# Row biases added on VectorE, a gating norm later in a bit search, and the first weight tiles of blocks three and four multiplied among the closing norms before them

## What is computed

```python
# block two (hybrid_layer)
proj = x @ w_in + b_in          # one bias per output column
ya = spatial_gating(gelu(a_u), gelu(a_v), a_ln_g, a_ln_b, a_ws, a_bs)   # layer norm of a_v over 256 columns
yc = dsa_attention(...)         # keeps the 256 best keys of each query (top_k), then softmax
km, vm = split(mem @ w_mem_kv, 2)
y = mixed @ w_out + b_out
x = layer_norm(DEEPNORM_ALPHA * x + y, ln_g, ln_b)
# block three: y = block(x @ w_in_3 ...) @ w_out_3;  x = layer_norm(ALPHA * x + y, ln1_g, ln1_b)
# feed-forward: a width-3 causal convolution over x @ w_up, gelu, product, @ w_down, layer norm
```

## Time and profile before

| | |
|---|---|
| three timed runs | 3071.8, 3079.6, 3080.2 us, median 3079.6 |
| profiled execution | 3074.3 us, its span 3072.2 us |
| TensorE busy in the span | 2867.8 us (93%), mean granted clock 0.975 |
| VectorE, ScalarE, GpSimd busy | 1721.1, 913.6, 554.6 us |

### The profile page before, as it was taken

How to read it: one execution, slowest core, us unless ns; L and a number is a source line. 1 busy time by engine, 2 the same in 40 slices (tenths; PEclk the granted TensorE clock), 3 DMA queues, 4 the chain that set the end, 5 groups by cost and what they waited for, 6 DMA issues and landing times. The chain is left out here.

```text
span 3072.2 us, 34403 instructions
## 1 busy us (share of the span) xinstructions
PE 2867.8 (93%) x13624; PEld 2299.5 (75%) x13624; DVE 1721.1 (56%) x2463; ACT 913.6 (30%) x1304; POOL 554.6 (18%) x274
## 2 busy tenths in 40 slices
PE   6899999999999999999998888999889999998997
PEld 3688888878887776678855677878677888886775
DVE  2699998655537642776987675782652233221032
ACT  2111112143324332322166512773411222212221
POOL 0000000000100010002100002442004443334664
PEclk9999999999999999999989899999999999999998
DMA  6111222224244530101110221001221111112342
GB/s 257 62 49 59 92 89 62 96 93 144 90 158 124 171 124 28 55 28 48 35 46 15 90 89 59 31 25 28 103 89 48 48 48 48 48 48 81 117 130 96
DMA packets 86643, 242.05 MB, mean 79 GB/s; under 512 B 6818, under 2 KB 33826, under 8 KB 84212
## 3 DMA queue, kind: packets, MB, share of 16 engines
q1 hardware_dynamic: 81620, 222.17, 21.9%
q10 hardware_dynamic: 4640, 17.30, 1.5%
q0 software_dynamic: 256, 0.82, 0.1%
HBM read 206.71 MB, written 33.55 MB: 78 GB/s over the span
## 5 line engine op out<-in xcount | busy, mean ns | idle before, releaser
L294 PE MATMUL pair<-u_hi,w_hi 128*128 128x512 f32 x768 | 300.7, 392 | 12.5 <-DVE w_lo L567 12.2
L516 DVE SCALAR_TENSOR_TENSOR conv_acc<-aT,cols,conv_acc 128x1024 f32<-128x1024 f32 x232 | 297.8, 1284 | 6.8
L296 PE MATMUL pair<-u_hi,w_lo 128*128 128x512 f32 x768 | 299.6, 390 | 0.0
L295 PE MATMUL pair<-u_lo,w_hi 128*128 128x512 f32 x768 | 299.5, 390 | 0.0
L294 PE MATMUL pair<-h_hi,up_hi 128*128 128x512 f32 x704 | 275.1, 391 | 7.4 <-POOL up_lo L289 7.4
L295 PE MATMUL pair<-h_lo,up_hi 128*128 128x512 f32 x704 | 274.8, 390 | 0.0
L296 PE MATMUL pair<-h_hi,up_lo 128*128 128x512 f32 x704 | 274.8, 390 | 0.0
L2564 DVE SCALAR_TENSOR_TENSOR ua<-pair,cols,ua 128x1023 f32<-128x1023 f32 x44 | 56.4, 1282 | 340.8 <-ACT ua L2548 340.8
L294 PEld LDWEIGHTS pair<-u_hi,w_hi 128*128 128x128 f32 x768 | 144.7, 188 | 43.5 <-DVE w_lo L567 12.4
L1663 DVE TENSOR_SCALAR_CACHE_REDUCE counted<-choice,top_i 128x384 uint8<-128x384 f32 (+2 forms) x192 | 168.9, 942 | 0.1
L295 PEld LDWEIGHTS pair<-u_lo,w_hi 128*128 128x128 f32 x768 | 144.7, 188 | 30.4 <-issue 0.5
(11 more groups left out here) (387 smaller groups left out, 6378.9 us busy)
## 6 DMA issues: line engine op xcount, KB each, us to landing
wt<-in_w_ch SPq DMA_DIRECT2D x60, 512.0 KB, 3.6
wo_raw<-in_w_out SPq DMA_DIRECT2D x48, 512.0 KB, 3.6
wt<-in_w_up SPq DMA_DIRECT2D x44, 512.0 KB, 3.4
wt<-in_w_down SPq DMA_DIRECT2D x44, 512.0 KB, 3.6
ada<-in_ada_w SPq DMA_DIRECT2D x8, 1536.0 KB, 8.0
wt<-in_w_conv SPq DMA_DIRECT2D x16, 512.0 KB, 3.6
qk<-qk_st SPq DMA_DIRECT2D x8, 1024.0 KB, 6.3
gates<-qk_st ACTq DMA_DIRECT2D x16, 512.0 KB, 2.6
```

The lines of the kernel that those rows point to most:

```text
L294: nc.tensor.matmul(bank, w[0], x[0], start=(first and k == 0), stop=False)
L295: nc.tensor.matmul(bank, w[0], x[1], start=False, stop=False)
L296: return nc.tensor.matmul(bank, w[1], x[0], start=False, stop=(last and k == n_k - 1))
L516: nc.vector.scalar_tensor_tensor(dst, x, w, conv_acc[:], ALU.mult, ALU.add).then_inc(conv_step, 1)
```

## The change

It has four parts.

1. **Row biases.** The 16 matmuls L1474 are gone. `b_row` is loaded to all 128 partitions, and VectorE takes each bank out with an addition of the bias. The eight of step 0 stand ahead of the logits, the eight of step 1 in the bit search, at places of the list `ROWS_AT` (two per search step: behind the third count and behind the sixth). ScalarE's copies are gone, and its Gelu stands behind the memory copies.
2. **Search.** `gate_norm` stands after step 22, the gating products after steps 29 and 30, and all 36 tie operations ahead of the attention.
3. **Block three.** `project_out` returns its engine programs; they run in the same block as the next stage. Behind the transposes of token tile 6, TensorE multiplies the first half (tokens 0 to 511) of weight tiles 0 and 1, into `pair[3]` and `pair[0]`; then come the transposes of token tile 7, then the second halves. The splits of these two weight tiles stand in the closing norm of block two: high on ScalarE ahead of its token loop, low on GpSimd. The block's end, the clearing of semaphores and the barriers between are gone; the pairs of the tiles of block three and the order of its last token tiles (`I_ORDER`) follow.
4. **Feed-forward.** The same with the first two tiles of `w_up`; GpSimd makes both of their parts during the closing norm of block three. Tiles 2 and 3 are written out ahead of the loops. The load of tile 3 waits until tile 1 is finished, since the low part of tile 1 lies in its slot.

```diff
+                if tail:
+                    pe.wait_ge(res_ok, TT - 1)
+                    pe.wait_ge(lo_ok, TT // 2)
+                    tail[0](pe)
                     if hT is not None:
                         transposes(TT - 1)
+                if tail:
+                    pe.wait_ge(lo_ok, TT)
+                    tail[1](pe)
...
-            sp.dma_start(b_row[:], a["b_row2"]).then_inc(b_in, 16)
+            sp.dma_start(b_row[:], bcast(a["b_row2"], 0, N_R2)).then_inc(b_in, 16)
...
-        N_TIES, TIES_AHEAD = 6 * (TT - 2), 24
+        N_TIES, TIES_AHEAD = 6 * (TT - 2), 36
...
-                    nc.tensor.matmul(bank, ones_row[:], b_row[:, c0:c1], start=False, stop=True).then_inc(row_mm, 1)
+                    last.then_inc(row_mm, 1)
...
+            ROWS_AT = [2, 4, 5, 6, 7, 9, 10, 11]
...
+            def row_evacuation(step, t):
+                c0, c1 = row_columns(1 - step)
+                j = step * TT + t
+                dve.wait_ge(row_mm, j + 1)
+                nc.vector.tensor_tensor(row2[:, t, c0:c1], row_bank(j)[:, 0:c1 - c0], b_row[:, c0:c1],
+                                        ALU.add).then_inc(row_ok, 1)
...
                 for t in range(2, TT):
                     count(n + 1, t, cand[:, t - 2:t - 1].bitcast(F32), ALU.is_ge)
+                    if t in (4, TT - 1) and 2 * n + (t > 4) in ROWS_AT:
+                        row_evacuation(1, ROWS_AT.index(2 * n + (t > 4)))
...
-                if n == 12:
+                if n == 22:
                     gate_norm()
-                if n in (26, 28):
-                    gate_product((n - 26) // 2)
+                if n in (29, 30):
+                    gate_product(n - 29)
...
-        clear_semaphores(keep=p3_w)
...
+                def first_tokens(pe):
+                    for w in range(2):
+                        pe.wait_ge(w3_lo, w + 1)
+                        for i in range(KT):
+                            tile_step(w, i)
+
+                def last_tokens(pe):
+                    for w in range(2):
+                        for i in range(KT, 2 * KT):
+                            tile_step(w, i)
+
+                second_out[1](pe, tail=(first_tokens, last_tokens))
...
+                third_out[0](sp)
+                for n in (2, 3):
+                    sp.wait_ge(*((up_split, 3) if n == 2 else (up_mm, 4)))
+                    sp.dma_start(wt[:, n % 2, :, :], a["w_up"][n, :, :].rearrange("p (k c) -> p k c", k=KT))\
+                        .then_inc(up_w[n % 2], 16)
...
+                for n in range(4):
+                    w_hi, w_lo = up_first[n] if n < 2 else [x[:, n % 2, :, :] for x in up_parts]
+                    pool.wait_ge(up_w[n % 2], 16 * (n // 2 + 1))
+                    if n >= 2:
+                        pool.wait_ge(third_mm, TT)
```

More of the change, by code:

```diff
@@ new lines, in evacuate, with run_scalar @@
+            def evacuate(act, t):
+                act.wait_ge(tr_mm, t + 1)
+                nc.scalar.activation((hT[0] if parts else hT)[:, :, t * P:(t + 1) * P],
+                                     flat(pair[2]).rearrange("p (k s) -> p k s", s=P), ACT.Copy).then_inc(tr_ok, 1)
+            def run_scalar(act, ahead=None):
+                for i, (to, src) in enumerate(vecs):
+                    act.dma_start(to[:], bcast(src, 0, D)).then_inc(vec_in, 16)
+                if split:
+                    act.wait_ge(*early)
+                    for n, k in enumerate(w_order):
+                        for i in range(len(w_loads)):
+                            if n == w_loads[i][2]:
+                                act.wait_ge(out_w[i], 16)
+                        nc.scalar.activation(split["w"][0][:, k, :], w_tile(k), ACT.Copy).then_inc(part_hi, 1)
+                        nc.scalar.activation(split["x"][0][:, k, :], split["raw"][:, k, :], ACT.Copy)\
+                            .then_inc(part_hi, 1)
+                if ahead:
+                    ahead(act)
+                for t in range(TT):
+                    if first_norm:
+                        act.wait_ge(res_ok, t + 1)
+                        nc.scalar.activation(tmp[:], xt[:, t % ring, :], ACT.Square, accum_out=sq_).then_inc(rms_sq, 1)
+                        act.wait_ge(rms_sq, t + 1)
+                        nc.scalar.activation(sd, sq_, ACT.Sqrt, bias=eps6[:], scale=1.0 / D).then_inc(norm_sd, 1)
+                    act.wait_ge(norm_in, t + 1)
+                    nc.scalar.activation(sd, mv_[:, 1:2], ACT.Sqrt, bias=eps5[:]).then_inc(norm_sd, 1)
+                    if t and hT is not None:
+                        evacuate(act, t - 1)
+                if hT is not None:
+                    evacuate(act, TT - 1)
@@ L1669, in mix_vector @@
             row_low(0, 1)
+            dve.wait_ge(b_in, 16)
+            dve.wait_ge(h2_out[0], 48)
+            dve.wait_ge(h2_out[1], 48)
+            for t in range(TT):
+                row_evacuation(0, t)
             dve.wait_ge(row_ok, TT)
@@ L2350, in _ @@
             def _(dve):
+                second_out[3](dve)
                 own = Count(dve, lb_dve)
```

373 lines of the change are left out of this document (188 added, 185 removed).

## The result

| | before | changed |
|---|---|---|
| timed runs, median | 3079.9 us (4 runs, 3071.8 to 3081.6) | 3023.6 us (4 runs, 3022.4 to 3026.4) |
| ratio | | 0.983, 95% interval 0.9817 to 0.9843 |
| span of the profiled execution | 3072.2 us | 3021.4 us |

A forecast was written before the change was run, and what follows sets the result against it. TensorE was taken as the bound, busy 2867.8 of 3072.2 us. Terms 16.8 + 3.7 + 2.8 + 16.0 + 15.0 - 1.5 - 1.5 = 51.3 off 3074.3 gave 3023.0; 2.7 for the executions' middle made 3026 us, range 3016 to 3043.

The forecast's parts named there:

- Row biases: Row steps 0 and 1: without the bias matmuls each of 16 row tiles falls by 1.05 us, 16.8 us won.
- Gelu: Ahead of the memory keys: ScalarE's activation moved behind the memory copies shortens TensorE's gap and avoids low clock, 3.7 us won.
- Ties: Attention's first items: VectorE's tie operations no longer hold up five items, which took 13.16 us instead of 10.35; 2.8 won.
- VectorE is not what ends here.: Search: VectorE's 47 us of saved waiting turn into only 2.8 us, since TensorE does not directly wait for it.
- Ends of the blocks: Ends of blocks two and three: first halves between token tiles 6 and 7's transposes win 16.0 and 15.0 us.
- Clock: The 2.46 us gap at each of two block ends: granted clock may fall behind it, 0 or 1.5, taken as 0.75.
- GpSimd beside VectorE: Block three's closing projection: four GpSimd parts slow VectorE's splits, 0.89 us each; 1.5 us lost, ends 0 and 5.4.
- The first: Both block ends: gaps come back smaller, clock falls, tiles 2 and 3 late, GpSimd holds VectorE; 3036 us, chance 15%.
- The second: Row step 1: VectorE's additions late at the banks, TensorE paced by the search; 3038 us, chance 12%.
- The third: Attention's first items stay slow from low clock though the ties go; 2.8 us missing, 3029 us, inside the forecast's range.
- fourth: Attention at low clock: 48 items at 3.66 us against 2.07 cost 76 us; slower, 3102 us, chance 4%.

## Why the prediction was right, and where it was not

The sum, 51.3, met 50.8 between the spans, the time 3026 met 3023.6. That the sum came so close is in part luck: GpSimd's term was 4.2 us too small, and two gains that were put at less or at nothing, the clock at the attention's start (2.0) and the closing norm of block two (2.2), made up for it. Term by term:

- **Row biases, 16.8.** Right, 16.6 (8 x 1.03 + 8.4), shown by putting them back (8.1 + 8.4). The bound of 1.22 for an addition was twice its 0.57, which cost nothing since it was cover anyway.
- **Gelu, 3.7.** Right in size, 4.0. The step took the clock as low for 2 us; by the 8.59 against 7.17 it cost 1.4, not 1.0. What the step didn't say: its new place is needed because of where the additions stand, 10.8 us and not 4.
- **Ties, 2.8.** Right, 2.8 with the search part alone. With the ties put back in the changed kernel the waits cost 2.6, and a fall of the clock behind them 1.7 more.
- **"VectorE is not what ends here."** This held for both kernels as they were built: the search part alone gives 4 us on the kernel before, and in the changed kernel VectorE is idle for 7.5 us ahead of the attention's first maxima. But it holds in the changed kernel only with the norm where it stands. TensorE is 12 to 19 us earlier there and the gating products three search steps later, and with the norm at step 12 it loses 15, at the gating product. I had costed the move against the old timing of TensorE only.
- **Ends of the blocks, 16.0 and 15.0.** Right: 25.4 and 25.5 us for the sequence against 25.26, where the clock didn't fall behind the gap.
- **Clock, 0.75 each.** Right as a mean: a gap of 2.4 us was followed by a fall in 8 of 18 cases, at 1.6 us each, which makes 0.7 per gap. In single profiles it is 0 or 1.6, and the profile of 3021.4 had none at either end.
- **GpSimd beside VectorE, -1.5.** The term that was mis-sized: -5.7. I took the 0.89 by which the addition of the earlier trace rows was longer as the price of a part. But that addition had begun when the part was half over, 1.38 of 2.41 us in; what the row says is that it could end only 1.1 us after the part did. Taken so, four parts shut VectorE out for their whole length. Four splits took 12.4 us (2164.28 to 2176.66) where 4.6 would do: 7.8 late, near the 8.5 that the four parts take alone (1.90 and 2.37, twice). The sum's other end, 5.4, is near the 5.7 by luck, for it was 9.6 us of delay less 4.2 of slack, all of it waiting. In the runs TensorE's wait is 3.0; it comes one inner tile sooner than at the last split, from which I had counted the slack. The other 2.7 are the low clock behind that wait, which I left out. The Trainium skill, GPSIMD Engine Reference, section 1 (Specifications), states that GpSimd contends with VectorE instructions that have two SBUF inputs. The traces agree: splits 2.92 and 3.41 us against 1.22, while an operation with one input in PSUM took 1.21 beside a part.
- **Rivals.** The first was half right (the collision, but not the late tiles: tile 2 is 0.3 us late). The second did not come: no wait of TensorE in row step 1, the additions keep the pace. The third and fourth did not come; there are, besides, only 16 cross items of the form that I priced, so the fourth would have cost 25 us by its own price, and could not have reached the other side.

## What to carry to other kernels

Read the start and the end of two operations that collide, not the duration of the one: an operation that begins in the middle of the other shows only the tail of the price. When a change makes the bounding engine earlier, redo the slack of every engine that it waits for against the new times; an edit that wins little alone can be what the others lean on. And when one part of a change is put back by itself, say what of the rest still depends on it: the loss is that of the mixture, not the part's own price. And where the last step of a stage waits for a chain of two other engines, cut the independent work that stands ahead of it in two, and keep as much of it behind the step as the chain lasts.

## What the runs showed of the hardware that was not expected

Two engines in turns on SBUF: a VectorE subtraction of two SBUF tensors, 1.22 us alone, took 2.92 and 3.41 beside GpSimd's, and GpSimd's own took 2.63 and 3.26 instead of the 1.90 and 2.37 that the same two took alone later in the profile. The first two of each took 7.05 us together (2163.47 to 2170.52), where 6.7 would do one after the other. GpSimd's second part, which took 3.26, ended 2.25 us behind VectorE's first long split (2169.45 and 2167.20), about the 2.37 that it takes alone: each seems to wait for the other's end. A gap of 2.4 us on TensorE was followed by a granted clock of 0.50 for some 3 us in 8 of 18 cases, in the same kernel at the same place now so, now not. Gaps of 1.15 us (ahead of the memory keys, all three profiles of the changed kernel) and 1.23 us (the kernel with one tile's parts held back) had full clock behind them; those of 2.92 to 3.06 us in block three's closing projection had 0.50 behind them in all three profiles.
